# Attention one head at a time: high and low halves stacked in the weights, and the softmax sum divided out of the output

## The reference, cut to what matters

```
s = einsum('nqhd,nkhd->nhqk', q, k) * HEAD_DIM ** -0.5      # 8 heads of 64
s = where(mask, s + bias[clip(dist)], -1e30)                # own chunk of 64 and the 8 chunks before
p = softmax(s, axis=-1)
att = einsum('nhqk,nkhd->nqhd', p, v)
h = h + concatenate([att, conv], -1) @ w_out
```

## Time and profile before

| | |
|---|---|
| median of three runs | 3165.56 us |
| span of the profiled execution | 3165.0 us |
| that execution and the median | 0.6 us apart: nothing of note lies around the span |
| TensorE busy, matmuls | 2913.1 us (92%) |
| VectorE busy | 2265.5 us (72%) |
| ScalarE busy | 1345.7 us (43%) |
| GpSimd busy | 1527.3 us (48%) |
| `attend` in the trace | 627.0 us (its first load) to 1108.65 us (first instruction of `finish`) |

### The profile page before, as it was taken

The page is one execution under the profiler, slowest core; times in us unless marked ns, Lnnn a source line. Parts: engine busy times, 40 slices in busy tenths (PEclk is TensorE's granted clock), DMA queues, the critical chain, the costliest instruction groups (busy, mean ns, idle before and its releaser), DMA issues.

```text
span 3165.0 us, 46365 instructions
## 1 busy us (share of the span) xinstructions
PE 2913.1 (92%) x14756; PEld 2733.9 (86%) x14756; DVE 2265.5 (72%) x2931; ACT 1345.7 (43%) x1940; POOL 1527.3 (48%) x738
## 2 busy tenths in 40 slices
PE   6998998788898879998999989999999999999997
PEld 6887887666676669998999989999989999899997
DVE  5655655546786667887688876788767887678876
ACT  4444444334554446233463334633345333454333
POOL 3434434369920035554555544555445554455554
PEclk9999999856988889999999999999999999999999
DMA  5654654654533243432534335343343433434333
GB/s 190 197 180 165 196 184 161 205 168 155 179 136 125 77 156 113 140 121 91 178 106 143 117 106 159 111 146 113 109 153 115 147 113 116 140 121 149 111 119 131
DMA packets 207048, 446.44 MB, mean 141 GB/s; under 512 B 63267, under 2 KB 114595, under 8 KB 206019
## 3 DMA queue, kind: packets, MB, share of 16 engines
q1 hardware_dynamic: 206947, 445.07, 41.7%
HBM read 384.32 MB, written 62.71 MB: 141 GB/s over the span
## 4 chain that ended last, share of the span: by engine, by line
issue 38%; POOL 23%; PE 2%; DVE 1%; POOLq 1%; ACT 0%; DVEq 0%; ACTq 0%
POOL c_w_lo L176 23%; PE c_acc L145 2%; POOLq L1043 0%; POOLq L175 0%; PE c_acc_p L145 0%; DVE c_csum L1220 0%; ACT c_w_hi L171 0%; PE c_ps_c L1373 0%; DVE c_csum L1229 0%; DVE c_crs L1233 0%; ACT c_uh L1137 0%; DVE y L1225 0%; DVE c_cx L1243 0%; DVE c_ml L1246 0%; DVE c_up L1290 0%
## 5 line engine op out<-in xcount | busy, mean ns | idle before, releaser
L176 POOL TENSOR_TENSOR c_w_lo<-c_w_raw,c_w_hi 128x1024 fp32r<-128x1024 f32 (+2 forms) x382 | 1065.6, 2790 | 1201.2 <-ACT c_w_hi L171 1200.9
L171 ACT ACTIVATE c_w_hi<-c_w_raw 128x1024 fp32r<-128x1024 f32 (+2 forms) x382 | 439.8, 1151 | 883.1 <-PE c_acc L145 866.3
L145 PE MATMUL c_acc<-c_uh,c_w_hi 128*128 128x416 f32 x2080 | 736.6, 354 | 37.3 <-DVE c_ul L1269 24.0
L145 PE MATMUL c_acc<-c_uh,c_w_lo 128*128 128x416 f32 x2080 | 738.3, 355 | 0.0
L145 PE MATMUL c_acc<-c_ul,c_w_hi 128*128 128x416 f32 x2080 | 729.9, 351 | 0.0
L1254 DVE SCALAR_TENSOR_TENSOR y<-gw,vec,y 128x416 f32<-128x416 f32 x600 | 460.3, 826 | 0.0
L145 PEld LDWEIGHTS c_acc<-c_uh,c_w_hi 128*128 128x128 f32 x2080 | 393.0, 189 | 46.6 <-DVE c_ul L1269 28.1
L176 POOL TENSOR_TENSOR a_w_lo<-a_w_raw,a_w_hi 128x1024 fp32r<-128x1024 f32 x102 | 246.1, 2412 | 369.2 <-ACT a_w_hi L171 369.2
L145 PEld LDWEIGHTS c_acc<-c_ul,c_w_hi 128*128 128x128 f32 x2080 | 393.7, 189 | 6.9 <-issue 0.8
L145 PEld LDWEIGHTS c_acc<-c_uh,c_w_lo 128*128 128x128 f32 x2080 | 393.1, 189 | 1.9
L145 PE MATMUL a_acc<-a_uh,a_w_hi 128*128 128x416 f32 x800 | 295.7, 370 | 27.9 <-POOL a_w_lo L176 21.2
(11 more groups left out here) (149 smaller groups left out, 4907.5 us busy)
## 6 DMA issues: line engine op xcount, KB each, us to landing
c_w_raw<-in_w_gu SPq DMA_DIRECT2D x220, 512.0 KB, 3.5
c_w_raw<-in_w_down SPq DMA_DIRECT2D x80, 704.0 KB, 4.0
a_w_raw<-in_w_in SPq DMA_DIRECT2D x104, 512.0 KB, 3.7
c_w_raw<-in_w_ple SPq DMA_DIRECT2D x40, 640.0 KB, 4.0
c_w_raw<-in_w_out SPq DMA_DIRECT2D x44, 512.0 KB, 3.7
c_h<-in_x SPq DMA_DIRECT2D x48, 208.0 KB, 3.1
gw<-o_g SPq DMA_DIRECT2D x78, 124.0 KB, 3.5
b_kh<-kh_d SPq DMA_DIRECT2D x6, 1536.0 KB, 6.8
```

Of the source, the lines that this page charges most:

```text
L145: mm = nc.tensor.matmul(out, w[wp](kw), u[up](ku), start=first and n == 0 and j == 0, stop=last and n == len(kts) - 1 and j == 2)
L171: self.nc.scalar.activation(self.hi[:, slot, 0:kts, :], self.raw[:, slot, 0:kts, :], ACT.Copy).then_inc(self.hi_done, 1)
L176: self.nc.gpsimd.tensor_tensor(self.lo[:, slot, 0:kts, :], self.raw[:, slot, 0:kts, :], self.hi[:, slot, 0:kts, :].bitcast(F32), ALU.subtr ...
```

## The change

Every head becomes an item of its own; there are 72 items (nine groups of eight heads), and each has two units (one in the sample). The units are the same 136.

- q is stored in memory as q2: for each head 64 rows of high part and below them 64 rows of low part. For that `project` makes four stores of 64 rows instead of two of 128. v is stored as v2, for each head 64 columns of high and 64 of low part, in one store instead of two.
- Scores: the weights are q2's 128 rows. The keys are loaded twice, into the upper and the lower 64 rows, so that one matmul with kh2 gives (q high + q low) times k high, and one with kl2 the same times k low: four matmuls a unit instead of six.
- The row of 640 is no longer multiplied with the inverse sum. DVE instead writes the inverse sum as 64 equal columns (line 750), PE transposes these once a unit (line 895), and the output is multiplied with the result.
- Product with v: v2 as weights gives the product with the high part in output rows 0 to 63 and with the low part in rows 64 to 127; two matmuls a tile instead of three, of 256 columns.
- Output: ACT copies rows 64 to 127 (vlow), DVE adds them to rows 0 to 63 (osum), DVE multiplies with the transposed inverse sum (att), ACT and DVE make the high and low part (ath, atl) as before.
- Loads: per item q2, kh2 twice, kl2 twice and v2, five items ahead, one after another in SP's queue with the stores. 
- There are no sections any more: one list of units, written out in full, with the product of the last item between the units of the next, also from group to group.

The diff, cut to its core (NS is 5, the items in flight; NR is 6):

```
-                        sp.dma_start(s["qk"[q] + "h"][rows, bass.ds(b * N, N)], znh[:, q, :].bitcast(F32)).then_inc(st_qk[q], 16)
-                        sp.dma_start(s["qk"[q] + "l"][rows, bass.ds(b * N, N)], znl[:, q, :].bitcast(F32)).then_inc(st_qk[q], 16)
+                        if q == 0:
+                            for hh in range(2):
+                                for part, src in ((0, znh), (HD, znl)):
+                                    r0 = (2 * m + hh) * P + part
+                                    sp.dma_start(s["q2"][r0:r0 + HD, bass.ds(b * N, N)],
+                                                 src[hh * HD:(hh + 1) * HD, q, :].bitcast(F32)).then_inc(st_qk[q], 16)
...
-        qh, ql = (sb(n, [P, HP, 2 * PQ], F32R) for n in ("qh", "ql"))
-        kh, kl = (sb(n, [P, 2, HP, WIN], F32R) for n in ("kh", "kl"))
-        vh, vl = (sb(n, [P, 2, GT, AW], F32R) for n in ("vh", "vl"))
+        q2 = sb("q2", [P, NS, 2 * PQ], F32R)
+        kh2, kl2 = (sb(n, [P, NS, WIN], F32R) for n in ("kh2", "kl2"))
+        v2 = sb("v2", [P, NS, GT, P], F32R)
...
+            def load(n):
+                it = items[n]
+                g, h, sl, got = it["g"], it["h"], n % NS, item_in[n % NS]
+                c0 = min(g, 8) * 2 * PQ
+                sp.dma_start(q2[:, sl, 0:it["wd"]].bitcast(F32),
+                             s["q2"][h * P:(h + 1) * P, c0:c0 + it["wd"]]).then_inc(got, 16)
+                hd = slice(h * HD, (h + 1) * HD)
+                if g < 8:
+                    short = it["first"] * P
+                    k0 = c0 - PAST + short
+                    for half in range(2):
+                        rows = slice(half * HD, (half + 1) * HD)
+                        for dst, src in ((kh2, s["kh"]), (kl2, s["kl"])):
+                            sp.dma_start(dst[rows, sl, short:WIN].bitcast(F32),
+                                         src[hd, k0:k0 + WIN - short]).then_inc(got, 16)
+                    sp.dma_start(v2[:, sl, it["first"]:GT, :].bitcast(F32),
+                                 s["v2"][k0:k0 + WIN - short, h * P:(h + 1) * P].rearrange(
+                                     "(t p) d -> p t d", p=P)).then_inc(got, 16)
+                else:
+                    hp, hh = divmod(h, 2)
...
+            for n in range(NS):
+                load(n)
             for ch in range(NCH):
                 gw_load(sp, t, c["gw"], 0, ch, gw_in)
+            for n in range(NI):
+                if n + NS < NI:
+                    sp.wait_ge(pv_done, n + 1)
+                    load(n + NS)
...
-                    nc.vector.reciprocal(rinv[0:mq, q:q + 1], rsum[0:mq, q:q + 1]).then_inc(rinv_done, 1)
-                    nc.vector.tensor_scalar(pr[0:mq, q, 0:w], pr[0:mq, q, 0:w], rinv[0:mq, q:q + 1], None,
-                                            ALU.mult).then_inc(pn_done, 1)
...
+                nc.vector.reciprocal(rinv[0:mq, i % NR, :],
+                                     rsum[0:mq, i % 3:i % 3 + 1].broadcast_to([mq, HD])).then_inc(rinv_done, 1)
...
+            def out_sum(n):
+                wd, q = items[n]["wd"], n % 2
+                dve.wait_ge(vlow_done, n + 1)
+                nc.vector.tensor_tensor(osum[:, q, 0:wd], ps_o[0:HD, q, 0:wd], vlow[:, q, 0:wd], ALU.add).then_inc(osum_done, 1)
+
+            def out_scale(n):
+                wd, q = items[n]["wd"], n % 2
+                dve.wait_ge(osum_done, n + 1)
+                nc.vector.tensor_tensor(att[:, q, 0:wd], osum[:, q, 0:wd], ps_o[0:HD, q, 2 * PQ:2 * PQ + wd],
+                                        ALU.mult).then_inc(att_done, 1)
+
+            def out_low(n):
+                wd, q = items[n]["wd"], n % 2
+                dve.wait_ge(ath_done, n + 1)
+                nc.vector.tensor_tensor(atl[:, q, 0:wd], att[:, q, 0:wd], ath[:, q, 0:wd].bitcast(F32),
...
+            def out_part(n):
+                wd, q = items[n]["wd"], n % 2
+                act.wait_ge(pv_done, n + 1)
+                if n >= 2:
+                    act.wait_ge(osum_done, n - 1)
+                nc.scalar.activation(vlow[:, q, 0:wd], ps_o[HD:P, q, 0:wd], ACT.Copy).then_inc(vlow_done, 1)
+
+            def out_high(n):
+                wd, q = items[n]["wd"], n % 2
+                act.wait_ge(att_done, n + 1)
+                if n >= 2:
+                    act.wait_ge(stored[q], 32 * (n // 2))
+                nc.scalar.activation(ath[:, q, 0:wd], att[:, q, 0:wd], ACT.Copy).then_inc(ath_done, 1)
+
...
-                        for j, (qt, kt) in enumerate(((qh, kh), (qh, kl), (ql, kh))):
-                            mm = nc.tensor.matmul(ps_s[0:mq, i % 2, a, 0:half], qt[part, ct, q0:q0 + mq],
-                                                  kt[part, sl, ct, keys], start=j == 0, stop=j == 2)
...
+                    nc.tensor.matmul(ps_s[0:mq, i % 2, a, 0:half], q2[:, sl, q0:q0 + mq], kh2[:, sl, keys],
+                                     start=True, stop=False)
+                    mm = nc.tensor.matmul(ps_s[0:mq, i % 2, a, 0:half], q2[:, sl, q0:q0 + mq], kl2[:, sl, keys],
+                                          start=False, stop=True)
...
-                        for j, (pt, vt) in enumerate(((pth, vh), (ptl, vh), (pth, vl))):
-                            mm = nc.tensor.matmul(ps_o[:, k % 2, :, q0:q0 + nq],
-                                                  vt[0:wd, u["slot"], a, u["hp"] * P:(u["hp"] + 1) * P],
-                                                  pt[0:wd, k % 2, a, :, q0:q0 + nq],
-                                                  start=x == 0 and j == 0, stop=x == n - 1 and j == 2)
...
+                if part == 0:
+                    pe.wait_ge(rinv_done, unit0[n] + per[n])
+                    if n >= 2:
+                        pe.wait_ge(att_done, n - 1)
+                    for p in it["pairs"]:
+                        mq = p["mq"]
+                        nc.tensor.transpose(ps_o[0:HD, q, 2 * PQ + p["j"] * PQ:2 * PQ + p["j"] * PQ + mq],
+                                            rinv[0:mq, (unit0[n] + p["j"]) % NR, :], c["ident"][0:mq, 0:mq])
+                    pe.wait_ge(ptl_done, 2 * (unit0[n] + per[n]))
+                for x in range(count * part // per[n], count * (part + 1) // per[n]):
+                    a, wd, q0, nq = todo[x]
+                    for j, pt in enumerate((pth, ptl)):
+                        mm = nc.tensor.matmul(ps_o[:, q, q0:q0 + nq], v2[0:wd, sl, a, :], pt[0:wd, q, a, q0:q0 + nq],
+                                              start=x == 0 and j == 0, stop=x == count - 1 and j == 1)
+                if part == per[n] - 1:
+                    mm.then_inc(pv_done, 1)
+
```

More of the change, by code:

```diff
@@ L635, in products @@
+        items = [item(n) for n in range(NI)]
+        us = [{**p, "n": it["n"], "h": it["h"], "q0": p["j"] * PQ, "w": sum(p["keys"]),
+               "last": p is it["pairs"][-1]} for it in items for p in it["pairs"]]
+        NU = len(us)
+        unit0 = [min(i for i, u in enumerate(us) if u["n"] == n) for n in range(NI)]
+        per = [len(it["pairs"]) for it in items]
+        def products(it):
+            ps_ = it["pairs"]
             if len(ps_) == 1:
@@ L830, in _ @@
+            for n in (NI - 2, NI - 1):
+                out_sum(n)
+                out_scale(n)
+                out_low(n)
         @block.scalar
         def _(act):
[L832 to L871 removed]
@@ new lines, in transposes @@
+            def transposes(i):
+                u = us[i]
+                mq = u["mq"]
+                pe.wait_ge(ex_done, i + 1)
+                for part, tiles, steps in parts(u):
+                    if i >= 1:
+                        pe.wait_ge(ptl_done, 2 * i + part - 1)
+                    for at, k in enumerate(tiles):
+                        wd = u["keys"][k]
+                        mm = nc.tensor.transpose(ps_t[0:wd, part, at * P:at * P + mq],
+                                                 pr[0:mq, i % 3, k * P:k * P + wd], c["ident"][0:mq, 0:mq])
+                    mm.then_inc(tr_done, steps)
@@ new lines, in values @@
+            def values(n, part):
+                it = items[n]
+                todo = products(it)
+                count, q, sl = len(todo), n % 2, n % NS
+                if part == 0:
[14 more added lines that the diff above has]
+                    mm.then_inc(pv_done, 1)
@@ new lines, in _ @@
+            for i in range(3):
+                scores(i)
+            for i in range(NU):
+                n = us[i]["n"]
+                transposes(i)
+                if i + 3 < NU:
+                    scores(i + 3)
+                if n:
+                    if per[n] == per[n - 1]:
+                        values(n - 1, us[i]["j"])
+                    else:
+                        for part in range(per[n - 1]):
+                            values(n - 1, part)
+            for part in range(per[NI - 1]):
+                values(NI - 1, part)
```

411 lines of the change are left out of this document (155 added, 256 removed).

## The result

The changed kernel takes 3202.9 us (median of 4 runs, 3199.2 to 3215.2) beside 3164.5 us of the kernel before on the same chip: ratio 1.0125, 95% interval 1.0104 to 1.0146. The forecast was 3088 us, range 3062 to 3136: wrong in sign. The profiled execution is the slowest of the four (3215.2 us, 12 us over the median); its span is 3212.9 us, 47.9 us over that of before (3165.0).

The account below looks back on a forecast made before the run. At full clock TensorE bounds attend, VectorE 0.4 us behind. 632.4 + 82 + 5 + 276 + 3 + 30 = 1028 us, plus 2 to `finish`: 1030 against 1108.65, -78 on 3165.0, so 3088 us, range 3062 to 3136.

Parts of the forecast that it names:

- Start of the block: Start of attend: six loads ahead of the first matmul, at 632.4 us, 7 us sooner; 5 us charged for item 5's loads.
- Units at 1.2 GHz: Groups 0 and 1 of attend at half clock: 2.57 us a unit instead of 2.92, 82 us instead of 94.
- the rival of a clock that stays down: Attend's TensorE clock never rises from 1.2 GHz: 3222 us; chance 0.08 for throughout or more than half, 0.03 for a third.
- The 4.3 us of a full unit at 1.2 GHz: TensorE's scores, product with v and transposes of a full attend unit at half clock: 4.3 us, against 4.9 before.
- Units at 2.4 GHz: Full attend units at full clock: VectorE next bound, 2.72 us of work, 2.88 us a unit, 276 us for 96.
- some 0.1 more: VectorE's extra time in full attend units beside GpSimd's convolution: some 0.1 us on top of 2.72.
- Transfers become the bound: Rival: attend's loads, slow at 64 rows, take 6.0 to 6.6 us an item, adding 12 to 40 us; chance 0.22.
- nothing changes: Attend's transfers at the rate of long rows: 2.9 us an item, within the 5.8 us an item has.
- SP issues 12 loads and 2 stores an item: Sample step: 14 issues at 0.43 us, 6 us an item; 22 us plus 8 to empty the output steps, 30.
- Project: Stage before attend: 3 us more of SP's issue time a block; bounds -5 and +6 us over five blocks, taken as 0.
- Section ends go altogether: Attend's full units follow without drain or clock fall; before, each loop turn paid about 18 us drain and 27 at half clock.

Follow-up runs that it names:

- run 3: The changed kernel without the loads for items 21 to 63, which compute with what stands in the buffers: 3166.9 us in a single run.
- run 11: The version of run 9 with the store of item n behind the load of item n+6 instead of ahead of it: 3065.1 us, ratio 0.9686.
- Runs 3 and 6: The second of these: the changed kernel with a head's keys fetched by one plain transfer of 128 neighbouring rows, not two of 64: 3159.0 us, single run.
- run 12: The changed kernel with only the store of item n moved behind the load of item n+6: 3183.4 us, ratio 1.0051.
- run 5: The changed kernel with the store of v cut into two of 512 columns (packets of 2048 bytes, not 4096): 3187.1 us, ratio 1.0065.
- run 4: The kernel before, with each of its two q stores a channel tile cut into two of 64 rows: 3170.6 us, ratio 1.0016.
- run 9: Changed kernel with k stored high over low, sample outputs before next scores, v store halved, common sample loads, zero rows under q low: 3093.2 us.

## Why the prediction was wrong

- **"Start of the block ... the first matmul at 632.4."** The start held: the first matmul came 5.5 us behind the first load, for 5.4. Its origin moved with `project`.
- **"Units at 1.2 GHz"**: the sum held, 92.4 us from first load to first full unit for 92, but by luck. TensorE waited 25.0 us for loads between 654 and 740 us, where 5 were charged, and its clock there was 0.64 on average, where 0.50 was reckoned with. The clock rose within group 1, as forecast, and the rival of a clock that stays down is out. The dips to 0.83 to 0.94 later stand beside waits for transfers; in run 3, without these, the clock is 1.00. The 4.3 us of a full unit at 1.2 GHz was not put to the test.
- **"Units at 2.4 GHz ... 2.72 ... 2.88 us a unit."** As work of the engines this was too high: 2.50 behind the convolution and 2.83 beside it, 2.70 over the stage (run 11; 259 us for 279). The single durations were right behind the convolution; they overlap (in run 3 those of a unit add up to 2.92 us in 2.48 us of busy time), so that adding them onto a busy time counts the overlap. Beside the convolution "some 0.1 more" was 0.33, all of it in `b_atl`. Before, the surplus there (61.17 of 68 us for 23 units, 2.66 us for 2.50) lay in the scaling of line 792, 787 ns for 589, which the change removes; read by instruction, the row would have said nothing of the new ones. In the kernel it was 3.1 to 3.2, because the step left the transfers at "nothing changes". *Transfers become the bound* had the right mechanism and, at 12 to 40 us, the right size for this stage; its chance of 0.22 looks too low now, and "the packets of 3072, 1024 and 512 B, nearer the first: 4 us" was the misjudged line: an item took 6.5 us. (By the rival's own terms, 4 us and 1.75 more for the keys are 5.75 and not 5.9.) Runs 3 and 6 show it; run 12 adds that 10 to 20 us of it are the order of load and store.
- **"SP issues 12 loads and 2 stores an item (6 us), five items ahead; the last three items may wait. 22 us, and 8 us to empty."** This is the largest fault and enough by itself to turn the sign: 104 us for 32. I took the prefetch of five items as given and never followed which wait in SyncE's queue stands ahead of a load. And 0.43 us an issue was read from the kernel before; nearly all loads of `attend` take 0.50 to 0.60 now, those of 128 rows too (`b_q` 0.58), and why, no run tells.
- **"Project ... Bounds -5 and +6 us; I take 0."** 20.9 us, far outside the bounds. The v store had "the same bytes in half the packets", and just that cost 17.4 us (run 5); the 3.6 us that are left are less than q's four stores alone cost in run 4 (6.6).
- **"Section ends go altogether"** held; narrower work and section ends together win 45.6 us over before from first load to sample (402.7 for 448.3). The sample and `project` took 71 and 21 us back.

Without these three faults the change comes out near what was forecast: run 11 takes 3065 us, 3.1% less than before. That is no proof of the forecast's sum, since run 11 also differs from the changed kernel in the roles of q and k, the rows of zeros and the sample's common loads.

## What to carry to other kernels

Where one in-order queue issues both stores and prefetches, write down for each load which store stands ahead of it and which later load that store waits for; the prefetch depth is what is left, and buffers alone don't give it. Price a transfer by its rows and its outermost dimension as well as its bytes, and a store by the queue it stands in. When a stage becomes short (32 queries instead of 128), count issues per item, since these don't shrink.

## What the runs showed of the hardware that was not expected

- Matmuls of 320 columns that alternate between 64 and 128 rows start every 0.34 us at the full clock; at equal heights, 64 rows (before) or 128 (run 9), every 0.15 us. 64 rows of zeros were cheaper, by 25 us of the kernel.
- A leading dimension of 2 in a transfer's pattern leaves 1.9 packets in flight where there were 12, and moves 81 GB/s; SyncE then spends 6 us in the issues of later, unrelated transfers.
- One store of 1664 KB in packets of 4096 bytes, once in each of five blocks, cost 17.4 us against two of 832 KB in packets of 2048.
- 64-row transfers slow the 512-byte packets of others beside them: 38 ns at the median for 27.
- A VectorE subtraction of 64x256 with both inputs in SBUF took 1.08 us while GpSimd's convolution ran and 0.41 us after it; with one input in PSUM it took 0.42 us in both.
